# The gated side of the one-hot rows in PEER routing: from VectorE and ScalarE to GpSimd

## What is computed

```python
qry = (xf @ w_query).reshape(T, PEER_HEADS, 2, PEER_DKEY // 2)
sa = jnp.einsum('thd,nd->thn', qry[:, :, 0], sub_keys_a)
sb = jnp.einsum('thd,nd->thn', qry[:, :, 1], sub_keys_b)
va, ia = lax.top_k(sa, PEER_TOPK)
vb, ib = lax.top_k(sb, PEER_TOPK)
cand = (va[..., :, None] + vb[..., None, :]).reshape(T, PEER_HEADS, PEER_TOPK * PEER_TOPK)
cand_idx = (ia[..., :, None] * PEER_NKEYS + ib[..., None, :]).reshape(T, PEER_HEADS, PEER_TOPK * PEER_TOPK)
top_s, pos = lax.top_k(cand, PEER_TOPK)
experts = jnp.take_along_axis(cand_idx, pos, axis=-1).reshape(T, PEER_HEADS * PEER_TOPK)
gates = jax.nn.softmax(top_s.astype(jnp.float32), axis=-1).reshape(T, PEER_HEADS * PEER_TOPK)
...
        act = jax.nn.gelu(jnp.einsum('tkd,td->tk', expert_u[eb], xb), approximate=False)
        return jnp.einsum('tk,tkd->td', gb * act, expert_v[eb])
```

## Time and profile before

| | us |
|---|---|
| median of 3 runs | 3937.39 |
| lowest and highest | 3934.48, 3939.39 |
| the profiled execution | 3936.05 |
| its span | 3934.3 |
| TensorE busy in the span | 3475.2 (88%) |
| VectorE busy | 2792.3 (71%) |
| ScalarE busy | 925.7 (24%) |
| GpSimd busy | 1469.0 (37%) |

### The profile page before, as it was taken

One profiled execution on the slowest core, in us unless ns is written; L12 is line 12 of the kernel. 1 busy time (PEld: TensorE's weight loads), 2 busy tenths in 40 slices (PEclk: granted clock), 3 DMA queues, 4 the chain that ended last, 5 costly groups with the idle time before them and its releaser, 6 DMA issues. The chain is left out here.

```text
span 3934.3 us, 39919 instructions
## 1 busy us (share of the span) xinstructions
PE 3475.2 (88%) x13263; PEld 1956.9 (50%) x13263; DVE 2792.3 (71%) x5246; ACT 925.7 (24%) x1903; POOL 1469.0 (37%) x1284
## 2 busy tenths in 40 slices
PE   7677999978888858896579999999999999999995
PEld 2443554335555558886434444444444444444442
DVE  1352457764566537888948889789897888877777
ACT  0052210004566402554521111111111111111110
POOL 1210004650000000000027666567656677676664
PEclk9787999986889879998689999999999999999998
DMA  9654325982111155754279999999999999899997
GB/s 345 253 212 141 121 86 219 376 312 108 46 43 38 19 189 201 260 202 163 86 293 360 377 387 378 354 391 386 379 369 378 391 392 381 341 405 390 383 369 258
DMA packets 350974, 1060.51 MB, mean 270 GB/s; under 512 B 31616, under 2 KB 90288, under 8 KB 344880
## 3 DMA queue, kind: packets, MB, share of 16 engines
q0 software_dynamic: 175936, 664.89, 44.2%
q1 hardware_dynamic: 174832, 393.05, 27.5%
HBM read 992.26 MB, written 65.31 MB: 269 GB/s over the span
## 5 line engine op out<-in xcount | busy, mean ns | idle before, releaser
L2788 PE MATMUL psH<-XT,e_uT 128*128 128x512 f32 x2048 | 930.9, 596 | 7.5 <-ACT e_uT L2825 7.5
L2801 PE MATMUL psY<-e_v,e_W 128*128 128x512 f32 x2048 | 881.5, 592 | 0.0
L2736 POOL DMA_INDIRECT pick_u<-in_expert_u,ids x512 | 669.7, 1308 | 386.0 <-DVE pick_dot L2902 272.8
L2918 DVE SCALAR_TENSOR_TENSOR acc<-pick_v,pick_w,acc 128x1024 f32<-128x1024 f32 x508 | 652.4, 1284 | 172.5 <-DMA pick_v<-in_expert_v,ids 130.9
L2744 POOL DMA_INDIRECT pick_v<-in_expert_v,ids x512 | 573.9, 1121 | 238.1 <-issue 146.0
L2902 DVE CUSTOM_DVE_ANT_0 e_junk<-pick_u,x_rows 128x1024 bf16<-128x1024 f32 x512 | 624.5, 1220 | 22.5 <-DMA pick_u<-in_expert_u,ids 10.6
L2801 PEld LDWEIGHTS psY<-e_v,e_W 128*128 128x128 f32 x2048 | 389.1, 190 | 489.8 <-issue 489.3
L2788 PEld LDWEIGHTS psH<-XT,e_uT 128*128 128x128 f32 x2048 | 370.8, 191 | 379.7 <-issue 369.2
L781 PE MATMUL ps_p<-w_in_sb,hT 128*128 128x512 f32 x896 | 393.7, 599 | 9.5 <-ACT stage L896 9.5
L2825 ACT ACTIVATE e_uT<-psU 128x512 f32<-128x512 f32 x256 | 152.1, 596 | 714.7 <-PE psU L2780 635.6
L781 PEld LDWEIGHTS ps_p<-w_in_sb,hT 128*128 128x128 f32 x896 | 170.8, 192 | 218.5 <-issue 208.1
(11 more groups left out here) (578 smaller groups left out, 4141.4 us busy)
## 6 DMA issues: line engine op xcount, KB each, us to landing
w_query_sb<-in_w_query SPq DMA_DIRECT2D x32, 2048.0 KB, 8.3
e_u<-in_expert_u SPq DMA_DIRECT2D x128, 512.0 KB
e_v<-in_expert_v SPq DMA_DIRECT2D x128, 512.0 KB
G_d<-G_stage SPq DMA_DIRECT2D x16, 2048.0 KB, 11.6
e_g<-G_d SPq DMA_DIRECT2D x16, 2048.0 KB
w_ada<-in_w_ada POOLq DMA_DIRECT2D x16, 1024.0 KB, 14.0
h_w_in<-in_w_in SPq DMA_DIRECT2D x7, 2048.0 KB, 15.5
w_in_sb<-in_w_in SPq DMA_DIRECT2D x7, 2048.0 KB, 16.6
```

The source lines that it names most:

```text
L2736: pool.indirect_dma_start(gu[:, i % NGU, :], None, io["expert_u"][0], bass.IndirectOffsetOnAxis(ids[:, q % 2, j:j + 1], 0)).then_inc(pu_in ...
L2788: m = pe.matmul(psH[a % 2][:, :], uT[:, a % 2, j, :], XT[:, j, :], start=j == 0, stop=j == KD - 1)
L2801: m = pe.matmul(psY[i % NY][:, :], W[:, (b * NBK + t) % NW, k * P:(k + 1) * P], v[:, t, half_cols(half)], start=t == 0, stop=t == NBK - 1)
L2918: dve.scalar_tensor_tensor(out=sums_q, in0=gv[:, i % NGV, :], scalar=wgt[:, m % 2, o:o + 1], in1=sums_q, op0=ALU.mult, op1=ALU.add).then_i ...
```

## The change

GpSimd makes `oa` complete. For each slot it waits for `kT_set` (in the first slot of a stage) and for `g_out` of slot i - 3, and then issues one `tensor_scalar` for each of the 8 tokens: `number` equal to the token's picks, times the token's gates, both taken per partition from `kT`. The last one signals `oa_set`. `hot` on VectorE makes `ob` alone, `gate_a` on ScalarE and the semaphore `oa_hot` are gone, and VectorE has one more `drain` at set-up, after the copy of `number`.

```diff
@@ -2310,7 +2310,7 @@
         q_out, q_copied, sc_out, sc_copied = sem("q_out"), sem("q_copied"), sem("sc_out"), sem("sc_copied")
         soft_v, soft_a, made, made_t, kT_set = sem("soft_v"), sem("soft_a"), sem("made"), sem("made_t"), sem("kT_set")
         hf_kept, sg_kept = sem("hf_kept"), sem("sg_kept")
-        oa_hot, oa_set, ob_set, g_out, g_kept = sem("oa_hot"), sem("oa_set"), sem("ob_set"), sem("g_out"), sem("g_kept")
+        oa_set, ob_set, g_out, g_kept = sem("oa_set"), sem("ob_set"), sem("g_out"), sem("g_kept")
         g_stored = [sem(f"g_stored{i}") for i in range(NS_)]
         block = ctx.enter_context(nc.Block())
 
@@ -2381,6 +2381,19 @@
             pool.drain()
             pool.sem_inc(set_up, 1)
 
+            def hot_gated(i, d, n):
+                if n == 0:
+                    pool.wait_ge(kT_set, d + 1)
+                if i >= NO:
+                    pool.wait_ge(g_out, i - NO + 1)
+                for t in range(GT):
+                    at = slice(n * GT + t, n * GT + t + 1)
+                    m = pool.tensor_scalar(oa[:, i % NO, t, :], number[:, :], kT[:, d % 2, 0, at], kT[:, d % 2, 2, at], ALU.is_equal, ALU.mult)
+                m.then_inc(oa_set, 1)
+
+            for i in range(ND * SLOTS):
+                hot_gated(i, i // SLOTS, i % SLOTS)
+
         @block.tensor
         def _(pe):
             pe.wait_ge(sub_in, 32)
@@ -2488,12 +2501,6 @@
                     act.wait_ge(sg_kept, 16 * nth_kept[k])
                 act.activation(scores(k)[:, 4 * g:4 * g + 4, :], psS[:, :].rearrange("p (j t) -> p j t", t=P), ACT.Copy).then_inc(sc_copied, 1)
 
-            def gate_a(i, d, n):
-                act.wait_ge(oa_hot, i + 1)
-                for t in range(GT):
-                    m = act.activation(oa[:, i % NO, t, :], oa[:, i % NO, t, :], ACT.Copy, scale=kT[:, d % 2, 2, n * GT + t:n * GT + t + 1])
-                m.then_inc(oa_set, 1)
-
             def keep(i):
                 q, t0 = i * GT // HT, i * GT % HT
                 act.wait_ge(g_out, i + 1)
@@ -2510,7 +2517,6 @@
                         if at == 0:
                             norm(i)
                     if j >= 1:
-                        gate_a((j - 1) * SLOTS + s, j - 1, s)
                         if s >= 1:
                             keep((j - 1) * SLOTS + s - 1)
                     for i, k, at in in_turn(j, s):
@@ -2529,6 +2535,7 @@
             dve.wait_ge(sub_t, 1)
             dve.tensor_copy(sub[:, :, :], psT[:, 0:2 * NK].rearrange("p (a n) -> p a n", a=2)).then_inc(sub_c, 1)
             dve.tensor_copy(number[:, :], number_i[:, :])
+            dve.drain()
             choose_start(dve, c)
 
             def norm_sum(i, k):
@@ -2567,9 +2574,8 @@
                 at = slice(n * GT, (n + 1) * GT)
                 if i >= NO:
                     dve.wait_ge(g_out, i - NO + 1)
-                for which, o, done in ((0, oa, oa_hot), (1, ob, ob_set)):
-                    dve.tensor_tensor(o[:, i % NO, :, :], number[:, :].unsqueeze(1).broadcast_to([P, GT, NK]),
-                                      kT[:, d % 2, which, at].unsqueeze(2).broadcast_to([P, GT, NK]), ALU.is_equal).then_inc(done, 1)
+                dve.tensor_tensor(ob[:, i % NO, :, :], number[:, :].unsqueeze(1).broadcast_to([P, GT, NK]),
+                                  kT[:, d % 2, 1, at].unsqueeze(2).broadcast_to([P, GT, NK]), ALU.is_equal).then_inc(ob_set, 1)
 
             def split():
```

## The result

| | before | after |
|---|---|---|
| median of 5 runs, us | 3934.48 | 3959.11 |
| lowest and highest | 3925.63, 3939.39 | 3955.13, 3966.16 |
| the profiled execution | 3936.05 | 3957.3 |
| its span | 3934.3 | 3955.6 |

The ratio is 1.0068, with a 95% interval of 1.0049 to 1.0087. The change makes the kernel slower by about 25 us. The forecast was 3896, faster by 41, with a range of 3878 to 3935. Rival (c) came about. Two executions of the experiments' tables, one of three of four slots (4456.9 us) and one of the kernel before (14256.94 us), were in a slower state; the ratios leave them out, and the medians of their rows hold them.

What follows compares the result with a forecast made beforehand. VectorE's instruction order was taken to bound routing, TensorE close behind in stages with two query tiles. Savings of 54.8 us less 13.3 for VectorE's waits left 41.5: 3894.6 against the profiled 3936.05, 3896 against the median; range 3878 to 3935.

Steps and rivals of the forecast that it cites:

- Rival (c): In routing, GpSimd is the bound and slower than what it replaces, TensorE waiting at `oa_set`; 3958 us at 0.66; chance 0.15.
- the sum: Savings in routing's four stages before GpSimd's own cost: 8.3 + 10.3 + 14.9 + 21.3 = 54.8 us.
- I take 0.45, nearest to the same tile: Assumed step of GpSimd's new operation in us: a select's 0.29 plus most of an empty instruction (0.175) for reading two values.
- The step T: Time for one of GpSimd's 512 new operations in routing; taken as 0.45 us, between 0.25 and 0.66.
- upper end of 0.66: Highest step in us allowed for GpSimd's operation: a select's cost at four times the elements, should compare and product go slowly.
- The charge for holding: GpSimd is stretched by all of VectorE's two-input time in routing: 36 us a stage.
- the forecast's own formula: Routing's length with GpSimd nearly the bound and every hold charged to it: 512T + 144 + 3 us against 464.
- point of decision, 0.62: Step in us of GpSimd's operation from which GpSimd, in front of each spread, makes routing slower than before.
- Rival (b): GpSimd is nearly the bound in routing: 20 us saved at T = 0.58, 3917; 3907 to 3933 between 0.56 and 0.61; chance 0.14.
- VectorE's own delay: VectorE's two-input operations in routing wait for GpSimd, 0.13 us each on the mean, 6.4 us a stage; 13.3 us count.
- What would show it: Signs for routing; right: GpSimd steps of 0.4 to 0.5 us, unchanged `hot_b`; wrong: steps over 0.55 or longer VectorE instructions.

Runs made afterwards that it cites:

- three of four slots: Against the kernel before, GpSimd makes the gated rows in three of four slots, VectorE and ScalarE those of the others; 3911.61 us, ratio 0.9928.

## Why the prediction was wrong

**What bounded the kernel before.** Right, VectorE's order first and TensorE close behind it in the first two stages. With GpSimd's share halved, 53.3 us of routing went, against 54.8 in the sum. That the two are so near is in part luck: the first two stages gave 4.4 more than the sum had for them, the last two 5.8 less, and VectorE was held a little, which this sum leaves out.

**The step that failed.** "I take 0.45, nearest to the same tile". The step T is 0.773 undisturbed (0.787 the operation's duration). Of the parts of that 0.45, the operands were put too high (0.16, where the step shows 0.07), and the rest was taken from the affine select: 0.29 us for fixed cost and streaming, where the runs show about 0.27 and 0.44. The forecast's upper end of 0.66 was drawn from the same wrong row, at four times the elements, so it was no upper end. The range stood on it: everything that T above 0.62 would do was outside of the range by the forecast's own choice, with a chance of 0.15.

**The charge for holding.** GpSimd was charged with all 144 us of VectorE's two-input time and lost 89, or 62%; the one operation that was taken out showed 71%. With both measured the forecast's own formula gives 396 + 89 + 3 = 488 us of routing, against 490.0: the form of the sum was right. With the full charge it would have given 543, so rival (c) as priced was too dear for its T, and its point of decision, 0.62, too low: with 89 us held it lies at (464 - 89 - 3)/512 = 0.73. The runs agree, with 25.4 us saved at a step of 0.70 and 26.1 lost at 0.773. Rival (b) was too dear as well: at T = 0.58 it had 20 us saved, and the run at 0.577 saved 40.5 in routing. There GpSimd was idle for 34 us waiting for TensorE, so it did not set the pace by itself.

**VectorE's own delay.** Forecast at 6.4 us a stage, 25.6 in four, with GpSimd busy for six tenths of the time, of which 13.3 were to count; measured some 10 in four with GpSimd busy all of it. The term was too large, and had no part in the result. (In its sum two stages of 6.4 are 12.8, not 12.3; nothing hangs on it.)

**Rival (c)** had the mechanism right: TensorE at `oa_set` behind GpSimd, VectorE behind `g_out`. That its time at 0.66, 3958 us, stands beside the 3959.11 measured is luck: T was larger and the charge for holding smaller. What spoke against it in the forecast, that the selects run at 0.94 ns for an element, was the fact that misled. The sentence on the page named there (the Trainium skill, GPSIMD Engine Reference, "Elementwise — side-by-side cycle accounting") would have led nearer, though still too low: its 2.6 cycles an element, which it explains by the two inputs of a `tensor_tensor`, are 2.2 ns by its clock. The runs show 3.4 ns with one input tile and two operations.

**What would show it.** The text named a step over 0.55 with TensorE waiting for `hot_a` on GpSimd, and VectorE's instructions longer. Both came.

## What to carry to other kernels

Price an operation on an engine that has not run it by rows of the same instruction, and where there are none, let the range reach to a multiple of the nearest row. On GpSimd two instructions over the same tile differed by a factor of 2.7. When work is moved to another engine, ask first how many operations it becomes there: one of VectorE for eight tokens (1.14 us) became eight of GpSimd (7.6). And when such a move makes the new engine the bound, moving less may be the way out, as it was here: with the gating left on ScalarE, the change gains 37 us where it lost 25.

## What the runs showed of the hardware

- GpSimd's `tensor_scalar` on 128x128 fp32: 0.787 us with two operands per partition and two operations, 0.597 with one of each, 0.641 with two constants, 0.574 at half of the width with two of each. One starts 0.773, 0.577, 0.70 and 0.554 us behind the other in these four, so constants save less of the pace than of the duration. A subtraction costs what a compare costs (788 ns against 787).
- Beside it, VectorE's operation with two SBUF inputs runs nearly as fast as alone (1252 ns against 1218), and GpSimd loses 0.89 us for each of 1.25. Without a two-input operation of VectorE beside it, none of 289 operations took over 0.802 us. The longest single operation of GpSimd took 3.9 us, five times its undisturbed time.
